# Six modulation chunks beside the linear attention: fp32 products replaced by products of fp32r parts, and a 4x2 matrix product in place of the turn

## The chip, the cores and the metric

One core of a Trainium2 chip runs the whole program. The metric is the device time in microseconds (us) of one execution. The engines are named as in the profile: PE (TensorE matmul), PEld (its weight load), DVE (VectorE), ACT (ScalarE), POOL (GpSimd) and SP (SyncE, which issues most of the loads).

## The reference, cut to what matters

Two transformer blocks on 512 tokens of width 1024 in float32. The first block takes its shifts, scales and gates from two conditioning vectors, `c` and `c_ctx`:

```
mod_x = (silu(c) @ w_ada[0] + b_ada[0])[:, None, :]      # w_ada: 1024 x 6144
mod_c = silu(c_ctx) @ w_ada[0] + b_ada[0]
sh1, sc1, g1, sh2, sc2, g2 = split(mod_x, 6)             # 1024 columns each
p_x = modulate(rmsnorm(h), sh1, sc1) @ w_in[0]           # also p_c, from ctx
... gla_bidir (4 heads, 2 directions, chunks of 64) ... pooling ...
h = h + g1 * (mix_x @ w_out[0])
h = h + g2 * moe(modulate(rmsnorm(h), sh2, sc2))         # top 4 of 32 experts
```

The second block (a retention and S5 mixer, differential attention, feed-forward layers) follows. `sh1` and `sc1` are needed at once. `g1`, `sh2`, `sc2` and `g2` are needed only from the output projection on, so the kernel computes most of them beside the linear attention.

## The kernel before, in words

**Modulations.** `w_ada` is cut into twelve chunks of 512 columns, c = 0 to 11. Each chunk comes in four loads of 512 KB (two blocks of 128 rows each). Chunks 0 to 3 come first. Chunks 4 to 9 are the ones that the change is about. Chunks 10 and 11 are computed in `out_pe`, at the start of the output projection. For a chunk `ada_pe` runs eight fp32 products: the stationary operand is `cc[:, k, :]` (128x2, the silu of both vectors), the moving one is the raw weight (128x512). The result is two rows of 512. `ada_act` copies them out of PSUM, `ada_pe` turns each 128 columns into a 128x2 block (four transposes of a 2x128 tile), and `add_ada` on DVE adds the bias.

**Parts.** Most other weights are used as fp32r parts. `conv_hi` (ACT, line 463) writes the high part of a unit of 128x1024 into one of four buffers of `wunits`. `conv_lo` (DVE, line 471) writes raw minus high over the raw weight in the ring. A high part may be written once PE has used the unit four places earlier, and a unit's ring slot is free for the next load once PE has used it.

**Ring.** SP loads the weights in the order in which they were planned into nine slots of 4 KB per partition. A load waits until PE has used what was in its slot, nine loads earlier. From the second half of `w_out` on, more slots come into use, and their first loads wait until POOL has finished its S5 tables (`"s5 parked"`).

**Steps.** The linear attention (`gla_pe`, `gla_act`, `gla_dve`) is four rounds (`ci` = 0 to 3: two pairs of heads, two directions). In each round every engine calls `step()` six times, at matching places. A step advances one generator of `jobs` and then one of `slow`, and each generator goes on to its next `yield`:

```
def step(self):
    if not self.advance(self.jobs) or self.pair:
        self.advance(self.slow)
```

The six places in a round are: before the turns of k (A), before the scores (B), before the masked product (C), after the first and after the second group of state products "u" (D, E), and before the output products "o" that read the states (F). DVE builds the states between the u products and the o products, with its steps at A, at B (before the mask), at C (before the decays of the next round), at D and E between the state updates, and at F after the decay products of the next round. The steps are numbered 1 to 24; after round 4 `finish_all` makes steps 25 and on, until both lists are empty. `jobs` holds the norm of the heads: DVE takes two reciprocals of 128x512 there, one in each of two steps.

The slow list is: pooling (steps 1 to 5), the S5 products (6 to 9), the modulation chunks 4, 5 and 6 (10 to 18, three steps each: two with four products each, one with the turn), the S5 turns (19 to 22), and the chunks 7, 8 and 9 (23 to 31). Instructions of an engine run in the order written, so a wait in a slow generator holds what stands behind it. PSUM banks are handed out in rotation, and a product waits until the former user of its bank has been read. In round 3 the last u products take the banks of the outputs of rounds 1 and 2, which the head norm frees on DVE.

After the linear attention `out_pe` runs chunks 10 and 11 and then the output projection; the router and the experts follow. ACT and DVE start on the parts of `w_out` after the barrier `"gla end"`.

Of the kernel before, what the change touches and what calls it, by code (L numbers as in the profile page):

```python
# [4 lines left out]
F32 = mybir.dt.float32  # L5
# [329 lines left out]
def build(nc, ins, out):  # L335
# [173 lines left out]
    for g in range(4):  # L509
        for h in range(2):  # L510
            W.plan(lambda g=g, h=h: I["ptab"][g, h * 256:(h + 1) * 256, :].rearrange("(j p) n -> p j n", p=128), 2, 512,
                   False)
    W.plan(lambda: I["w_pool"][0].rearrange("g c d -> c g d"), 4, 128, False)
    for c in range(4, 10):
        plan_cols(W, w_ada, 8, c * 512, 512, False)
    U_IN = len(W.units)
    plan_cols(W, w_ada, 8, 5120, 512, False)
    plan_cols(W, I["w_out"][0], 8, 0, 512)
# [359 lines left out]
    def ada_dve(v, c):  # L878
        yield
        yield  # L880
        add_ada(v, c)
        yield

    def add_ada(v, c):
        v.wait_ge(*pe("adat", c))
        v.own()
        v.inc(v.e.tensor_tensor(
            mcol[:, 4 * c:4 * c + 4, :], bank_of(("adat", c))[:, 0:8].rearrange("p (j s) -> p j s", s=2),
            C("bada", 4 * c, 4).unsqueeze(2).to_broadcast([128, 4, 2]), ALU.add), ("ada", c))
        v.free(("adat", c))  # L890

    RAW_ADA = [4 * FIRST.index(c) if c < 4 else 25 + 4 * (c - 4) for c in range(12)]

    def ada_row(c):
        return ar[0:2, c * 512:c * 512 + 512] if c < 4 else ar[0:2, 22272:22784]

    def mod_act(q):
        q.limit = U_IN
        q.wait_ge(*dve("all", "cols"))
        q.act(cc[:, :, 0], C("c", 0, 8), ACT.Silu)  # L900
        q.act(cc[:, :, 1], C("cctx", 0, 8), ACT.Silu, "silu c")
        sumsq_act(q, "x", hk, 8, 512, sq1)
        root2_act(q, "x", rx)
        sumsq_act(q, "ctx", lambda k: HC[:, k, :], 8, 256, sq1)
        root2_act(q, "ctx", rc)
        for h in range(2):
            for c in (h, h + 2):
                for _ in ada_act(q, c):
                    pass
            q.wait_ge(*dve("gm", h))  # L910
            for k in range(4 * h, 4 * h + 4):
                for s in range(2):
                    q.act((HXh, HCh)[s][:, k, :], normed_in(s, k), ACT.Identity, ("hn high", s, k), bias=M(0, k, s), scale=gm[:, k, s:s + 1])
            for u in (2 * h, 2 * h + 1):
                conv_hi(q, W, u)
# [18 lines left out]
            pass  # L934

    def mod_dve(v):
        v.limit = U_IN
        root1_dve(v, "x", 8, 512, rx, 1.0 / 1024)
        root3_dve(v, "x", rx)
        root1_dve(v, "ctx", 8, 256, rc, 1.0 / 1024)  # L940
        root3_dve(v, "ctx", rc)
        for k in range(8):
            v.stt(XN[:, k, :], hk(k), C("nmix", k), rx, ALU.mult, ALU.mult)
            v.stt(HC[:, k, :], HC[:, k, :], C("nmix", k), rc, ALU.mult, ALU.mult)
        for h in range(2):
            for c in (h, h + 2):
                for _ in ada_dve(v, c):
                    pass
            v.ts(gm[:, 4 * h:4 * h + 4, :], mcol[:, 8 + 4 * h:12 + 4 * h, :], 1.0, None, ALU.add, None, ("gm", h))
            ahead = None  # L950
            for k in range(4 * h, 4 * h + 4):
                for s in range(2):
                    v.ts(ntmp[s][k % 2], normed_in(s, k), gm[:, k, s:s + 1], M(0, k, s), ALU.mult, ALU.add)
                    if ahead:
                        hn_low(v, *ahead)
                    ahead = (s, k)
            hn_low(v, *ahead)
            for u in (2 * h, 2 * h + 1):
                conv_lo(v, W, u)
# [930 lines left out]
            yield  # L1890

    def out_act(q):
        q.limit = None
        for u in range(NUNIT):
            conv_hi(q, W, U_IN + u)
            split_act(q, "mix", mixp, lambda k: MX[:, k, :], range(2 * u, 2 * u + 2))
        q.wait_ge(*pe("ada", 10))
        q.copy(ada_row(10), bank_of(("ada", 10))[0:2, :], ("ada", 10))
        q.free(("ada", 10))
        q.slow += [last_ada_act(q), shift_act(q)]  # L1900
        tile = lambda c, m: q.jobs.append(tile_act(q, c * 4 + m))
        dense(q, conv_hi, W, [512], 8, tile)
        by_tiles(q, 1, tile)
        q.u += 4

    def out_dve(v):
        v.limit = None
        v.ts(gm2, mcol[:, 32:40, 0], 1.0, None, ALU.add, None)
        v.tt(gm2, gm2, C("nmlp", 0, 8), ALU.mult, "gm2")
        v.copy(S3[:, :, 0].bitcast(F32R), mcol[:, 24:32, 0])  # L1910
# [9 lines left out]
        v.u += 4  # L1920

    def out_pe(p):
        tails = [ada_pe(p, c) for c in (10, 11)]
        for x in tails:
            next(x)
# [1827 lines left out]
    def program_pe(p):  # L3753
# [3 lines left out]
        p.slow, p.pair = [s5_small_pe(p)], True  # L3757
        proj_pe(p)
        all_wait(p, "proj")
        p.slow += [pool_pe(p), s5_large_pe(p), ada_pe(p, 4), ada_pe(p, 5), ada_pe(p, 6), s5_turn_pe(p)]  # L3760
        p.slow += [ada_pe(p, c) for c in range(7, 10)]
        gla_pe(p)
        out_pe(p)
        p.pair = False
# [31 lines left out]
    def program_act(q):  # L3796
# [3 lines left out]
        q.slow, q.pair = [s5_small_act(q)], True  # L3800
        proj_act(q)
        all_wait(q, "proj")
        q.slow += [pool_act(q), s5_large_act(q), ada_act(q, 4), ada_act(q, 5), ada_act(q, 6), s5_turn_act(q)]
        q.slow += [ada_act(q, c) for c in range(7, 10)]
        gla_act(q)
        out_act(q)
        q.pair = False
# [35 lines left out]
    def program_dve(v):  # L3843
# [3 lines left out]
        v.slow, v.pair = [s5_small_dve(v)], True  # L3847
        proj_dve(v)
        all_wait(v, "proj")
        v.slow += [pool_dve(v), s5_large_dve(v), ada_dve(v, 4), ada_dve(v, 5), ada_dve(v, 6), s5_turn_dve(v)]  # L3850
        v.slow += [ada_dve(v, c) for c in range(7, 10)]
        gla_dve(v)
        out_dve(v)
        v.pair = False
# [132 lines left out]
```

## Time and profile before

| | us |
|---|---|
| median of 3 runs | 3272.61 (3269.02 to 3274.2) |
| the profiled execution, device time | 3273.05 |
| its span, first to last instruction | 3271.0 |
| PE busy | 3063.2 (94% of the span) |
| DVE busy | 2143.3 (66%) |
| ACT busy | 1645.5 (50%) |

The span is 2.05 us shorter than the device time of the same execution. The linear attention with what runs beside it takes the stretch from 206 to 358 us of the span; the output projection's products begin at 376.7 us.

### The profile page before, as it was taken

How to read it: one execution, taken by the hardware profiler on the slowest of the kernel's cores; microseconds unless marked ns; L12 is line 12 of the kernel's file. 1: busy time of each engine (PE TensorE's matmuls, PEld its weight loads, DVE VectorE, ACT ScalarE, POOL GpSimd, SP SyncE). 2: the span in 40 equal slices, each digit the busy share in tenths (PEclk: the TensorE clock that was granted, in tenths of full speed). 3: DMA queues.
4: the chain of work that ended last, by engine and by line, in shares of the span. 5: the costliest groups of instructions: out<-in, count | busy, mean ns of one | idle time of the engine just before them, and what ended most of it. 6: DMA issues, size and time to landing. Idle time of an engine off the chain costs nothing.

```text
span 3271.0 us, 37073 instructions
## 1 busy us (share of the span) xinstructions
PE 3063.2 (94%) x13794; PEld 2400.9 (73%) x13794; DVE 2143.3 (66%) x2483; ACT 1645.5 (50%) x1948; POOL 261.3 (8%) x234
## 2 busy tenths in 40 slices
PE   7989989999999999999979978999998987999998
PEld 3856467777777777777757756888886764888887
DVE  4555449999999999999966444443446457443446
ACT  2332328878887788878853212332335237432334
POOL 1053720000000000000010000000000000000000
PEclk8998969999999999999988978999999988999999
DMA  6244749999999999999963212223232210223210
GB/s 214 70 132 154 228 156 377 362 377 375 378 364 374 376 376 370 365 378 375 367 203 127 84 35 88 90 91 103 90 110 74 83 58 1 84 90 103 90 65 26
DMA packets 225086, 643.11 MB, mean 197 GB/s; under 512 B 20054, under 2 KB 38516, under 8 KB 224036
## 3 DMA queue, kind: packets, MB, share of 16 engines
q1 hardware_dynamic: 207984, 577.70, 48.7%
q0 software_dynamic: 12816, 51.39, 5.6%
q10 hardware_dynamic: 4100, 11.59, 0.9%
q8 instruction: 110, 1.80, 0.2%
q14 instruction: 76, 0.62, 0.1%
HBM read 608.10 MB, written 32.51 MB: 196 GB/s over the span
## 4 chain that ended last, share of the span: by engine, by line
PE 83%; DVE 11%; ACT 3%; issue 2%; DMA 1%; DVEq 0%; ACTq 0%; SPq 0%; POOLq 0%
PE ps L272 79%; PE ps L288 3%; DVE arena L203 2%; DVE arena L192 2%; ACT wunits L463 2%; DVE ring_r L471 1%; DVE arena L199 1%; ACT arena L237 1%; DVE arena L215 1%; DVE arena_r L203 1%; DVE arena L211 1%; DMA arena<-in_ctx 1%; DVE arena_r L471 1%; DVE arena L197 0%; DVE H L192 0%
## 5 line engine op out<-in xcount | busy, mean ns | idle before, releaser
L471 DVE TENSOR_TENSOR ring_r<-ring,wunits 128x1024 fp32r<-128x1024 f32 x795 | 948.7, 1218 | 660.2 <-ACT wunits L463 636.4
L463 ACT ACTIVATE wunits<-ring 128x1024 fp32r<-128x1024 f32 x795 | 834.6, 1054 | 809.0 <-PE ps L272 797.1
L272 PE MATMUL ps<-arena_r,wunits 128*128 128x512 f32 (+1 forms) x3552 | 1110.3, 394 | 12.4 <-DVE arena_r L192 6.9
L272 PE MATMUL ps<-wunits,arena_r 128*128 128x512 f32 x3520 | 991.3, 399 | 7.0 <-DVE arena_r L192 7.0
L272 PEld LDWEIGHTS ps<-arena_r,wunits 128*128 128x128 f32 x3552 | 671.4, 190 | 160.9 <-issue 16.6
L272 PEld LDWEIGHTS ps<-wunits,arena_r 128*128 128x128 f32 x3520 | 658.7, 189 | 152.2 <-DVE arena_r L192 8.8
L272 PE MATMUL ps<-arena_r,ring_r 128*128 128x512 f32 (+1 forms) x1776 | 694.8, 391 | 0.0
L272 PE MATMUL ps<-ring_r,arena_r 128*128 128x512 f32 x1280 | 410.3, 391 | 0.0
L272 PEld LDWEIGHTS ps<-arena_r,ring_r 128*128 128x128 f32 x1776 | 337.1, 190 | 70.4
L471 DVE TENSOR_TENSOR arena_r<-arena,wunits 128x1024 fp32r<-128x1024 f32 x240 | 284.9, 1221 | 16.6 <-ACT wunits L463 9.4
L463 ACT ACTIVATE wunits<-arena 128x1024 fp32r<-128x1024 f32 x240 | 254.3, 1061 | 65.6 <-PE ps L272 63.6
L272 PEld LDWEIGHTS ps<-ring_r,arena_r 128*128 128x128 f32 x1280 | 241.2, 188 | 53.1 <-issue 2.2
L272 PE MATMUL ps<-arena 128*128 128x128 f32 (+11 forms) x1074 | 192.4, 365 | 42.2 <-DVE arena L207 16.1
L237 ACT ACTIVATE arena<-ps 128x512 f32<-128x512 f32 (+6 forms) x190 | 121.3, 639 | 198.2 <-PE ps L272 144.9
L272 PEld LDWEIGHTS ps<-arena 64*128 64x128 f32 (+5 forms) x1074 | 135.0, 202 | 99.8 <-issue 41.4
L288 PE MATMUL ps<-KC,arena 128*128 128x128 f32 (+3 forms) x854 | 129.5, 294 | 82.5 <-DVE arena L203 43.5
L288 PEld LDWEIGHTS ps<-KC,arena 128*128 128x128 f32 (+3 forms) x854 | 104.1, 153 | 116.5 <-DVE arena L203 61.7
L272 PE MATMUL ps<-arena_r 128*128 128x512 f32 (+3 forms) x520 | 160.0, 392 | 0.9 <-DVE arena_r L197 0.9
L237 ACT ACTIVATE arena<-arena 128x512 f32<-128x512 f32 (+6 forms) x155 | 80.0, 516 | 134.1 <-DVE arena L192 84.1
L2360 POOL DMA_INDIRECT sum_scratch<-arena x33 | 52.3, 1586 | 1037.4 <-ACT arena L237 1037.4
L192 POOL TENSOR_TENSOR ring<-ring 128x512 f32<-128x512 f32 (+5 forms) x90 | 105.5, 1172 | 195.4 <-DVE ring L192 142.4
L192 DVE TENSOR_TENSOR arena<-ps,arena 128x512 f32<-128x512 f32 (+1 forms) x115 | 78.7, 684 | 61.3 <-PE ps L272 51.2
(171 smaller groups left out, 1936.1 us busy)
## 6 DMA issues: line engine op xcount, KB each, us to landing
ring<-in_w_gu SPq DMA_DIRECT2D x382, 512.0 KB, 8.5
ring<-in_w_down SPq DMA_DIRECT2D x170, 512.0 KB, 6.4
arena<-in_w_gu SPq DMA_DIRECT2D x146, 512.0 KB, 8.6
arena<-in_w_down SPq DMA_DIRECT2D x94, 512.0 KB, 6.4
ring<-in_w_ada SPq DMA_DIRECT2D x48, 512.0 KB, 4.5
ring<-in_ffn_w_gate SPq DMA_DIRECT2D x44, 512.0 KB, 3.5
ring<-in_ffn_w_up SPq DMA_DIRECT2D x44, 512.0 KB, 3.6
ring<-in_ffn_w_down SPq DMA_DIRECT2D x40, 512.0 KB, 3.6
```

The lines of the kernel that those rows point to most:

```text
L192: self.inc(self.e.tensor_tensor(o, x, y, op), key)
L199: self.inc(self.e.tensor_scalar(o, x, s1, s2, op0, op1), key)
L203: self.inc(self.e.scalar_tensor_tensor(out=o, in0=x, scalar=s, in1=y, op0=op0, op1=op1), key)
L211: self.inc(self.e.reciprocal(o, x), key)
L215: self.inc(self.e.tensor_reduce(o, x, AX.X, op), key)
L237: self.inc(self.e.activation(o, x, f, **kw), key)
L272: ins = self.e.matmul(o, l_, r_, start=start, stop=stop, skip_group_check=True)
L288: ins = self.e.transpose(o, x, self.ident[0:k, 0:k])
L463: q.inc(q.e.activation(h, raw, ACT.Copy), (st.tag, "hi", i))
L471: q.inc(q.e.tensor_tensor(lo, raw, h.bitcast(F32), ALU.subtract), (st.tag, "lo", i))
L2360: g.e.indirect_dma_start(out=sum_d, out_offset=bass.IndirectOffsetOnAxis(ap=idx, axis=0), in_=YB[i], in_offset=None, compute_op=ALU.add).t ...
```

## The change

Chunks 4 to 9 are planned as units (`split`), so ACT makes a high part and DVE a low part of each of their 24 pieces. The two vectors of `cc` are split as well: `CPARTS` holds for each block of 128 rows four columns, the high parts of both and the low parts of both. A chunk takes 16 fp32r products (128x4 stationary, 128x512 moving): the four columns with the weight's high part and with its low part. The result is four rows. The turn is four fp32 products of a 4x128 tile with `pick`, a 4x2 matrix that adds the row of high parts and the row of low parts. The high parts of the next chunk are written after the copy of the present one. For chunk 4 there are two more steps ahead, in which ACT and DVE make its first parts.

```diff
+    U_ADA = len(W.units)
     for c in range(4, 10):
-        plan_cols(W, w_ada, 8, c * 512, 512, False)
+        plan_cols(W, w_ada, 8, c * 512, 512)
     U_IN = len(W.units)
...
+    CPARTS = r(22816, 32, 4)
+    pick = ar[0:4, 22848:22850]
+    def ada4_pe(p, c):
+        if c == 4:
+            yield
+            yield
+        key = ("ada", c)
+        b = p.bank(key)
+        p.inuse.append(b)
+        if c == 4:
+            p.wait_ge(*dve("c parts"))
+        for j in range(4):
+            u = W.units[ada_unit(c, j)]
+            h, _, lo = unit_tiles(u)
+            p.wait_ge(*W.lo(u.i))
+            if j == 0:
+                p.claim(key)
+            for k in range(2):
+                kk = 2 * j + k
+                p.mm(PB[b][0:4, :], CPARTS[:, kk, :], h[:, k * 512:(k + 1) * 512], kk == 0, False)
+                p.mm(PB[b][0:4, :], CPARTS[:, kk, :], lo[:, k * 512:(k + 1) * 512], False, kk == 7, None, k == 1)
+            p.note((W.tag, "used", u.i))
+            if j == 1:
+                yield
+        p.note(key)
+        p.inuse.remove(b)
+        yield
+        b = p.bank(("adat", c))
+        p.wait_ge(*act("ada", c))
+        p.claim(("adat", c))
+        for j in range(4):
+            p.mm(PB[b][:, 2 * j:2 * j + 2], ar[0:4, 22272 + j * 128:22400 + j * 128], pick, j == 0, j == 3,
+                 ("adat", c) if j == 3 else None)
+        yield
+    def ada4_act(q, c):
+        def high(c, j0):
+            for j in range(j0, j0 + 2):
+                conv_hi(q, W, ada_unit(c, j))
+        if c == 4:
+            q.limit = U_IN
+            q.act(CPARTS[:, :, 0:2], cc, ACT.Copy, "c high")
+            high(c, 0)
+            yield
+            high(c, 2)
+            yield
+        yield
+        q.wait_ge(*pe("ada", c))
+        if c > 4:
+            q.wait_ge(*pe("adat", c - 1))
+        q.copy(ar[0:4, 22272:22784], bank_of(("ada", c))[0:4, :], ("ada", c))
+        q.free(("ada", c))
+        if c < 9:
+            high(c + 1, 0)
+        yield
+        if c < 9:
+            high(c + 1, 2)
+        yield
+    def ada4_dve(v, c):
+        def low(c, j0):
+            for j in range(j0, j0 + 2):
+                conv_lo(v, W, ada_unit(c, j))
+        if c == 4:
+            v.limit = U_IN
+            v.tt(pick, ident[0:4, 0:2], ident[0:4, 2:4], ALU.add)
+            v.wait_ge(*act("c high"))
+            v.tt(CPARTS[:, :, 2:4], cc, CPARTS[:, :, 0:2].bitcast(F32), ALU.subtract, "c parts")
+            yield
+            low(c, 0)
+            yield
+        low(c, 2)
+        yield
+        yield
+        if c < 9:
+            low(c + 1, 0)
+        add_ada(v, c)
+        yield
...
-        p.slow += [pool_pe(p), s5_large_pe(p), ada_pe(p, 4), ada_pe(p, 5), ada_pe(p, 6), s5_turn_pe(p)]
-        p.slow += [ada_pe(p, c) for c in range(7, 10)]
+        p.slow += [pool_pe(p), s5_large_pe(p), ada4_pe(p, 4), ada4_pe(p, 5), ada4_pe(p, 6), s5_turn_pe(p)]
+        p.slow += [ada4_pe(p, c) for c in range(7, 10)]
```

The slow lists of ACT and DVE change in the same way, and the counters of units at `mod_act`, `mod_dve`, `out_act`, `out_dve` and `out_pe` are set to the new numbering. The order of the loads and their sizes stay as they were.

## Rows read from the trace of the kernel before

**Rows 1.** The page's first part: busy time and share of each engine.
```profile
PE 3063.2 (94%) x13794; PEld 2400.9 (73%) x13794; DVE 2143.3 (66%) x2483; ACT 1645.5 (50%) x1948; POOL 261.3 (8%) x234
```
**Rows 2.** Windows of round 3 and the tail: length, PE, PEld, DVE, ACT, POOL, clock, DMA.
```profile
290.00:316.00 26.00, 20.23 (x93) 12.25 (x94) 20.48 (x26) 3.54 (x6) 1.20 (x2) 0.76 0.56 199
...
340.00:358.00 18.00, 16.64 (x45) 3.86 (x46) 12.55 (x10) 4.00 (x6) 17.22 (x11) 1.00 0.57 190
```
**Rows 3.** Timeline of PE, a chunk's products, fp32r triples and small products (start, length).
```profile
341.83 7.03 PE L272 MATMUL ps<-ring,SM 128*2 128x512 f32 x16
379.51 0.62 PE L272 MATMUL ps<-arena_r,wunits 128*128 128x512 f32 x2
379.96 0.39 PE L272 MATMUL ps<-arena_r,ring_r 128*128 128x512 f32 x1
380.19 0.62 PE L272 MATMUL ps<-arena_r,wunits 128*128 128x512 f32 x2
405.12 0.95 PE L272 MATMUL ps<-KC,arena 128*128 128x2 f32 x8
```
**Rows 4.** Groups by form, 236 to 377 us: the parts on DVE and ACT, the copy.
```profile
L471 DVE TENSOR_TENSOR ring_r<-ring,wunits 128x1024 fp32r<-128x1024 f32 x4 | 4.9, 1218 | 0.0
L463 ACT ACTIVATE wunits<-ring 128x1024 fp32r<-128x1024 f32 x4 | 4.2, 1044 | 0.7 <-DVE MOD L887 0.7
L237 ACT ACTIVATE arena<-ps 2x512 f32<-2x512 f32 x7 | 4.1, 586 | 33.2 <-PE ps L272 33.1
```
**Rows 5.** Timeline of PE, rounds 2 and 3; in brackets idle time and its releaser.
```profile
260.88 3.60 PE L272 MATMUL ps<-ring,SM 128*2 128x512 f32 x8
...
271.73 5.14 PE L272 MATMUL ps<-arena 64*128 64x64 f32 x32 [1.27 <-DVE arena L203]
276.81 5.09 PE L272 MATMUL ps<-ring,SM 128*2 128x512 f32 x8
...
306.36 1.22 PE L272 MATMUL ps<-arena 64*128 64x256 f32 x4 [4.64 <-DVE BPT L192]
...
309.22 6.29 PE L272 MATMUL ps<-arena 64*128 64x64 f32 x32 [1.13 <-DVE arena L203]
```
**Rows 6.** Timeline of DVE, rounds 2 and 3: decays, states, mask, head norm.
```profile
258.92 2.67 DVE L192 TENSOR_TENSOR arena<-arena 128x768 f32<-128x768 f32 x2
...
262.15 1.51 DVE L203 SCALAR_TENSOR_TENSOR arena<-arena,ps 128x256 f32<-128x256 f32 x3
...
289.07 1.58 DVE L1678 COPY_PREDICATED arena<-arena,ps 128x512 f32<-128x512 uint32 x2 [3.92 <-PE ps L272]
...
290.95 1.68 DVE L192 TENSOR_TENSOR arena<-arena 128x768 f32<-128x768 f32 x2
...
295.12 3.35 DVE L211 RECIPROCAL arena<-arena 128x512 f32<-128x512 f32 x1
...
302.22 3.35 DVE L211 RECIPROCAL BPT<-BPT 128x512 f32<-128x512 f32 x1
```
**Rows 7.** Timeline of PE, the end of round 4 and the tail.
```profile
336.26 3.39 PE L272 MATMUL ps<-arena 64*128 64x64 f32 x32
...
357.57 0.41 PE L288 MATMUL ps<-KC,arena 2*128 2x2 f32 x4 [0.68 <-ACT arena L237]
357.91 10.46 PE L272 MATMUL ps<-ring,SM 128*2 128x512 f32 x24
371.44 5.29 PE L272 MATMUL ps<-ring,SM 128*2 128x512 f32 x8 [3.07 <-DMA ring<-in_w_ada]
```
**Rows 8.** Timeline of POOL: its products, tables and the end of its S5 work.
```profile
258.26 31.40 POOL L192 TENSOR_TENSOR ring<-ring 128x512 f32<-128x512 f32 x24 [46.02 <-PE ps L272]
...
327.85 32.75 POOL L192 TENSOR_TENSOR ring<-ring 128x32 f32<-128x32 f32 x36
...
370.00 0.10 POOL L223 MEMSET ring<- 128x16 f32 x1 [8.52 <-DMA s_ww<-ring]
```

**Rows 9.** Timeline of ACT: the first part of the second half of `w_out`.
```profile
382.49 1.06 ACT L463 ACTIVATE wunits<-ring 128x1024 fp32r<-128x1024 f32 x1 [14.37 <-PE ps L272]
```

More of the change, by code:

```diff
@@ L882, in ada_dve, with ada_unit @@
         yield
+    CPARTS = r(22816, 32, 4)
+    pick = ar[0:4, 22848:22850]
+    def ada_unit(c, j):
+        return U_ADA + 4 * (c - 4) + j
+    def ada4_pe(p, c):
[30 more added lines that the diff above has]
+        yield
@@ L890, in add_ada @@
         v.free(("adat", c))
-    RAW_ADA = [4 * FIRST.index(c) if c < 4 else 25 + 4 * (c - 4) for c in range(12)]
+    RAW_ADA = [4 * FIRST.index(c) if c < 4 else 25 + 4 * (c - 10) for c in range(12)]
     def ada_row(c):
@@ L897, in mod_act @@
     def mod_act(q):
-        q.limit = U_IN
+        q.limit = U_ADA
         q.wait_ge(*dve("all", "cols"))
@@ L936, in mod_dve @@
     def mod_dve(v):
-        v.limit = U_IN
+        v.limit = U_ADA
         root1_dve(v, "x", 8, 512, rx, 1.0 / 1024)
@@ L1892, in out_act @@
     def out_act(q):
-        q.limit = None
+        q.limit, q.u = None, U_IN
         for u in range(NUNIT):
@@ L1906, in out_dve @@
     def out_dve(v):
-        v.limit = None
+        v.limit, v.u = None, U_IN
         v.ts(gm2, mcol[:, 32:40, 0], 1.0, None, ALU.add, None)
@@ L1922, in out_pe @@
     def out_pe(p):
+        p.u = U_IN
         tails = [ada_pe(p, c) for c in (10, 11)]
@@ L3802, in program_act @@
         all_wait(q, "proj")
-        q.slow += [pool_act(q), s5_large_act(q), ada_act(q, 4), ada_act(q, 5), ada_act(q, 6), s5_turn_act(q)]
-        q.slow += [ada_act(q, c) for c in range(7, 10)]
+        q.slow += [pool_act(q), s5_large_act(q), ada4_act(q, 4), ada4_act(q, 5), ada4_act(q, 6), s5_turn_act(q)]
+        q.slow += [ada4_act(q, c) for c in range(7, 10)]
         gla_act(q)
@@ L3849, in program_dve @@
         all_wait(v, "proj")
-        v.slow += [pool_dve(v), s5_large_dve(v), ada_dve(v, 4), ada_dve(v, 5), ada_dve(v, 6), s5_turn_dve(v)]
-        v.slow += [ada_dve(v, c) for c in range(7, 10)]
+        v.slow += [pool_dve(v), s5_large_dve(v), ada4_dve(v, 4), ada4_dve(v, 5), ada4_dve(v, 6), s5_turn_dve(v)]
+        v.slow += [ada4_dve(v, c) for c in range(7, 10)]
         gla_dve(v)
```

## Prediction

> **What bounds the kernel now.** I read the page first: PE is busy for 94% of the span [rows 1], so work taken from PE should be worth having, if PE is what the stage waits for. So next the windows of the linear attention: in round 3 (290 to 316 us) DVE is busy for 20.5 of 26 us and PE for 20.2, at a clock of 0.76 [rows 2]. The reader is to see that in this stretch DVE, not PE, has the fuller hand. The timeline of PE says the same by its waits: the last u products of round 3 wait 4.64 us and the o products of round 3 wait 1.13 us, both for DVE, and behind that wait the o products take 6.29 us where those of round 4 take 3.39 [rows 5, 7]. The clock explains this: 1.2 GHz after the idle time, 2.4 GHz in round 4. The timeline of DVE shows what it does meanwhile: mask, decays, two reciprocals of 3.35 us and the states, without a gap [rows 6]. After round 4 comes a tail, from 339.65 us (336.26 + 3.39) to 357.91, in which chunks 8 and 9 run bare on PE and only a copy of 0.6 us stands between them [rows 4, 7].
>
> **What the change takes off PE.** A chunk takes 7.03 us now, and three fp32r products of 512 columns take 0.68 us (379.51 to 380.19), so 0.227 each and 3.63 for sixteen [rows 3]. That is 3.4 us less a chunk, 20.4 for six. The new turn is not in the trace: at least the 0.41 of the present one [rows 7], at most the 0.95 of four fp32 products of 128 by 2 [rows 3]. I take 0.95, as it has the same instructions and no transposing; that gives back 3.2. Sum on PE: -17.2 us.
>
> **What it adds.** 24 high parts on ACT of 1.044 us (25.1) and 24 low parts on DVE of 1.218 us (29.2) [rows 4], in a stretch of about 100 us. The splitting of `cc` and `pick` are three small instructions, under 0.5 us on each engine, in step 10. The loads are the same and in the same order. ACT has room (4.0 of 18 us in the tail, 3.5 of 26 in round 3) [rows 2]. DVE has none in round 3. The order matters more than the sums: chunk 4 gets two empty steps, so every chunk comes two steps later on PE. Chunk 4 lies in steps 12 to 14, chunk 5 in 15 to 17, chunk 6 in 18 to 20, the S5 turns in 21 to 24, and chunk 7, which today lies within round 4, falls wholly behind it.
>
> **Round 2.** Nothing differs until 260.88 [rows 5]. Then PE has no chunk to fill steps 10 and 11 and ends its u products near 263. Its next step needs the first low part. DVE has three state updates until 263.7, four more (0.5 each [rows 6]), and then makes two low parts: PE gets them at 267.4 and 268.6. After 4.5 us idle I expect PE at 1.2 GHz, so chunk 4's first eight products take up to 3.4 us instead of 1.8, and the o products start near 270.8 and not at 271.73. At that clock they end near 276.5, the low parts of the second half come behind the decay products at 277.5 to 279, and chunk 4 ends at 280. Today the first half of chunk 5 ends at 281.9 (276.81 + 5.09) [rows 5]. So round 2 gains 2 us, with half a chunk less done.
>
> **Round 3.** On DVE the low parts of chunk 5 stand ahead of the mask and behind it, and the first ones of chunk 6 ahead of the last state updates. The mask today begins at 289.07 after 3.92 us idle, so that pair is half hidden (the mask starts at about 287.6, as PE is 2 us early), the two others are not. DVE then runs: mask to 289.2, two low parts to 291.7, decays to 293.4, states, first reciprocal and four states to about 302.5, second reciprocal to 307.4, two low parts to 310, last states by 312. On PE the turn of chunk 5 now takes the bank that the second head norm frees, near 307, the last u products stand behind it, and then the first half of chunk 6 (up to 3.4 us at 1.2 GHz) stands ahead of the o products. These start near 313.9, against 309.22 [rows 5]: 4.7 us later.
>
> **Round 4.** Today 339.65 - 309.22 = 30.4 us from these o products to the last ones' end, of which 7.0 are chunk 7. Without it 23.4; the second half of chunk 6 adds 1.8 to 3.4, its dearer turn 0.5, the low parts of chunk 7 ahead of the mask about 1.2. So 27.2, and the last o products end at 341.1 instead of 339.65: **+1.5 us**. PE's 3.4 us for each of chunks 4 to 6 are spent on waits for DVE and the lower clock.
>
> **The tail.** From that end T: chunk 7 (1.8), the head norm's sums (1.9), chunk 7's second half: T+5.9 with some delay of the squares on ACT behind the last S5 copies. Only then are the high parts of chunk 8 made, since they stand behind the copy of chunk 7. So each chunk is a chain over three engines: copy 0.6, high 1.04, low 1.22 four times, product 0.9, that is 7.6 us, which is no less than the 7.03 + 0.6 + 0.4 of today. DVE also does the head norm in the same steps. From its first reciprocal to its second lie 7.1 us, with four states (2.0) among them, so a half of the head norm is 4.9 [rows 6]; one half stands ahead of the low parts 8.2 and 8.3, the other ahead of 9.0. Chain: T+7.6 high part, T+10 two low parts, T+14.9 norm, T+17.4 two low parts, T+18.3 chunk 8; second norm until T+22.3, four low parts until T+27.2, products and copy T+28.8, turn and some twenty handovers of 0.05: T+30.8. Today it is 18.3. **+12 us** (12.5 rounded down, as the squares may not be late).
>
> **POOL beside it.** POOL computes on 128x512 tiles from 258.26 to 289.7 and again from 327.85 to 360.6 [rows 8]. Two 768-column differences on DVE take 2.67 us in the first stretch and 1.68 outside it [rows 6], 0.5 us more for each. Eight low parts stand one behind another in the tail, and POOL's second stretch starts about 9 us later than today (the S5 turns end two steps later) and so covers them all. Bounds: nothing, or 0.5 for each (+4). I take **+2.5**. The Trainium skill (page "SBUF — State Buffer", section "Who interferes with whom") says that a DVE instruction with two SBUF inputs and a POOL instruction that reads SBUF hold the shared ports in turns for a whole instruction. By that rule the low parts, whose inputs both lie in SBUF, would wait too; the pair of differences agrees (2.67 against 1.68), and the sum would be +4 instead of +2.5.
>
> **After the tail.** Today the last load of chunk 11 makes PE wait 3.07 us [rows 7]; after the change PE begins chunk 10 at 1.2 GHz (about +3) and that wait is covered: even. POOL's end, today at 370.00, lets the second half of `w_out` be loaded [rows 8], and it is first used at 382.49 [rows 9]: 12 us of room, while POOL slips by 9 to 15 and PE by 16. Everything behind follows PE. **Sum: 1.5 + 12 + 2.5 = +16 us.** Against the profiled 3273.05 that is 3289; this execution is 0.44 above the median of 3272.61, so **3288.6 us**.
>
> **Rivals.** *Chain of the tail shorter (no change that can be measured).* DVE waits less than I think in rounds 3 and 4 (T at 335) and POOL costs nothing: -4.7 + 12 = +7, and with the norms placed in the gaps of the copies (2.4 off each) +2: 3275 to 3280. For it speaks that DVE has much idle time ahead of round 3's mask [rows 6]; against it the instruction order. *PE's work decides (faster).* If the parts come early enough that PE never waits for one, -17.2 stands: 3255.4. It decides as soon as each low part is done before PE reaches its product; for it speak the 94% of PE [rows 1], against it the order in which the next chunk's high parts stand behind the present chunk's copy. *POOL and clock (slower still).* If each low part in the tail waits for a POOL instruction of about 1 us and PE stays at 1.2 GHz through chunks 8 to 10, +8 + 6 on top of 13.5: 3300.
>
> **From this to the numbers.** A measurement of this kernel tells about 0.2%, 6.5 us, from no change. Forecast (3280 to 3297): 0.58. No measurable change (3266 to 3279): 0.2. Faster, at PE's sum or part of it: 0.1. Slower still (3297 to 3305): 0.12. So slower 0.7, same 0.2, faster 0.1. Range 3268 to 3299: it leaves out the faster case and the end of the last one.
>
> **What would show it.** A chunk of 16 products with 3.6 us of PE where it isn't waiting; a wait of PE for DVE's line 471 before each half of chunks 8 and 9; reciprocals between low parts 8.1 and 8.2; the o products of round 3 near 314 and the end of round 4 near 341; chunk 10 near 374. Wrong it would be if DVE reached the low parts of chunk 8 ahead of the reciprocal's step, or if the products with four columns took another time than those with 128.

## The result, and the profile after

The changed kernel takes 3307.37 us (median; 3302.37 to 3316.61), the kernel before in the same session 3272.45. The ratio is 1.0108, with a 95% interval from 1.0091 to 1.0124. A second session of the same kernel gave 1.0113 [1.0094, 1.0132]. So the change costs 1.1%, some 35 us: the sign is the one forecast, the size is twice the 16 us. The profiled execution is the fastest of its runs (3302.37, span 3300.2) and lies 29.2 us above the span before.

The page's first part, after. PE is busy for only 4.7 us less than in [rows 1]; DVE and POOL are busy for 41.7 and 13.6 us more.
```profile
PE 3058.5 (93%) x13818; PEld 2401.7 (73%) x13818; DVE 2185.0 (66%) x2509; ACT 1669.1 (51%) x1973; POOL 274.9 (8%) x234
```
Groups of instructions by form of the changed kernel, from 255 to 388 us (DVE) and to 420 us (ACT): the low and the high parts. The high part costs what it did in [rows 4], 1042 against 1044 ns. The low part does not: its mean is 1802 ns where [rows 4] has 1218, so 24 of them take 42.3 us and not the 29.2 of the forecast.
```profile
L471 DVE TENSOR_TENSOR ring_r<-ring,wunits 128x1024 fp32r<-128x1024 f32 x24 | 42.3, 1802 | 7.7 <-ACT wunits L463 7.7
...
L463 ACT ACTIVATE wunits<-ring 128x1024 fp32r<-128x1024 f32 x29 | 28.7, 1042 | 20.1 <-PE ps L272 17.9 <-DVE MOD L976 2.2
```
Timeline of DVE after, in order: the low parts (pairs, L471), with the decay products (L203, 128x512) and the reciprocals between. The pairs beside POOL's first stretch take 3.49, 4.28, 4.01 and 2.64 us, and those of the tail 3.21, 5.12, 5.89 and 4.22. Undisturbed, a pair is 2.35 (the row at 320.53). The reciprocals stand at 3.35 everywhere, as in [rows 6].
```profile
265.67 3.49 DVE L471 TENSOR_TENSOR ring_r<-ring,wunits 128x1024 fp32r<-128x1024 f32 x2
...
273.74 3.11 DVE L203 SCALAR_TENSOR_TENSOR arena<-arena 128x512 f32<-128x512 f32 x2
276.77 4.28 DVE L471 TENSOR_TENSOR ring_r<-ring,wunits 128x1024 fp32r<-128x1024 f32 x2
...
287.19 4.01 DVE L471 TENSOR_TENSOR ring_r<-ring,wunits 128x1024 fp32r<-128x1024 f32 x2
...
293.06 2.64 DVE L471 TENSOR_TENSOR ring_r<-ring,wunits 128x1024 fp32r<-128x1024 f32 x2
...
307.83 3.35 DVE L211 RECIPROCAL BPT<-BPT 128x512 f32<-128x512 f32 x1
...
319.19 1.42 DVE L203 SCALAR_TENSOR_TENSOR arena<-arena 128x512 f32<-128x512 f32 x2
320.53 2.35 DVE L471 TENSOR_TENSOR ring_r<-ring,wunits 128x1024 fp32r<-128x1024 f32 x2
...
354.44 3.21 DVE L471 TENSOR_TENSOR ring_r<-ring,wunits 128x1024 fp32r<-128x1024 f32 x2 [2.80 <-ACT wunits L463]
...
357.95 3.35 DVE L211 RECIPROCAL arena<-arena 128x512 f32<-128x512 f32 x1
...
362.74 5.12 DVE L471 TENSOR_TENSOR ring_r<-ring,wunits 128x1024 fp32r<-128x1024 f32 x2
367.89 3.35 DVE L211 RECIPROCAL BPT<-BPT 128x512 f32<-128x512 f32 x1
...
372.67 5.89 DVE L471 TENSOR_TENSOR ring_r<-ring,wunits 128x1024 fp32r<-128x1024 f32 x2
...
378.77 4.22 DVE L471 TENSOR_TENSOR ring_r<-ring,wunits 128x1024 fp32r<-128x1024 f32 x2
```
Timeline of POOL after. Its two stretches are 5.2 and 7.3 us longer than in [rows 8]: the contention is mutual. The second begins at 340.75 and ends at 380.77, so seven of the tail's eight low parts start beside it; the last one runs from 381.78 and takes 1.21.
```profile
256.84 36.63 POOL L192 TENSOR_TENSOR ring<-ring 128x512 f32<-128x512 f32 x24 [46.02 <-PE ps L272]
...
340.75 40.02 POOL L192 TENSOR_TENSOR ring<-ring 128x32 f32<-128x32 f32 x36
```
Instruction by instruction (the timeline of both engines in windows of 0.1 us), three of POOL's products of the tail and the low part that starts beside each of them:
```profile
372.12 2.45 POOL L192 TENSOR_TENSOR ring<-ring 128x1024 f32<-128x1024 f32 x1
372.67 2.98 DVE L471 TENSOR_TENSOR ring_r<-ring,wunits 128x1024 fp32r<-128x1024 f32 x1
...
374.65 2.82 POOL L192 TENSOR_TENSOR ring<-ring 128x1024 f32<-128x1024 f32 x1
375.58 2.98 DVE L471 TENSOR_TENSOR ring_r<-ring,wunits 128x1024 fp32r<-128x1024 f32 x1
...
377.55 3.22 POOL L192 TENSOR_TENSOR ring<-ring 128x1024 f32<-128x1024 f32 x1
378.77 3.09 DVE L471 TENSOR_TENSOR ring_r<-ring,wunits 128x1024 fp32r<-128x1024 f32 x1
```
The three low parts end 1.08, 1.09 and 1.09 us after the end of the POOL product beside them (375.65 against 374.57, 378.56 against 377.47, 381.86 against 380.77). Alone a low part takes 1.22 us. So each stands until the POOL product under way is done and then takes 1.1 us more. It becomes 1.8 to 1.9 us longer here. Beside the products of 512 columns in the first stretch (1214 ns each in the kernel before) the low parts become 0.3 to 1.1 longer.
Timeline of PE after: first product with chunk 4's parts, o products of rounds 2, 3 and 4, chunk 7's turn, chunk 8's second half and its turn, then chunks 10 and 11 with the wait for the last load. (An fp32 product stands in the trace as two entries, an fp32r product as one; so 24 entries are chunk 10 and half of chunk 11.) A product of fp32r parts with 512 columns takes 0.23 us from start to start at 2.4 GHz and 0.43 at 1.2 GHz, whether its stationary tile has 4 columns or 128; a turn takes 1.05 and 1.86.
```profile
267.31 0.58 PE L272 MATMUL ps<-wunits,arena_r 128*4 128x512 f32 x1 [6.05 <-DVE ring_r L471]
...
271.01 3.67 PE L272 MATMUL ps<-arena 64*128 64x64 f32 x32
...
319.32 3.41 PE L272 MATMUL ps<-arena 64*128 64x64 f32 x32
...
340.68 3.98 PE L272 MATMUL ps<-arena 64*128 64x64 f32 x32 [0.62 <-DVE arena L203]
...
353.45 1.05 PE L272 MATMUL ps<-arena 4*128 4x2 f32 x8 [0.68 <-ACT arena L237]
...
365.07 0.59 PE L272 MATMUL ps<-wunits,arena_r 128*4 128x512 f32 x1 [5.50 <-DVE ring_r L471]
...
370.45 1.86 PE L272 MATMUL ps<-arena 4*128 4x2 f32 x8 [0.68 <-ACT arena L237]
...
387.95 12.00 PE L272 MATMUL ps<-ring,SM 128*2 128x512 f32 x24
405.30 4.99 PE L272 MATMUL ps<-ring,SM 128*2 128x512 f32 x8 [5.35 <-DMA ring<-in_w_ada]
```
The last o products end at 344.66 (339.65 before), chunk 10 starts at 387.95 (357.91, [rows 7]) and is turned at 415.91 (382.32 before). The waits of PE between 240 and 420 us, summed by what ended them, say what that time was:
```profile
PE ps L272 <- DVE ring_r L471: 26.0, 11, 6.0
PE ps L272 <- DVE BPT L192: 6.3, 1, 6.3
PE ps L272 <- DVE arena L192: 5.6, 1, 5.6
PE ps L272 <- DMA ring<-in_w_ada: 5.4, 1, 5.4
```
With three small groups these waits are 47.3 us; the same view of the kernel before sums to 12.0. So PE waits 35.3 us longer in a stage that became 35.0 longer (173.9 from the o products of round 1 to the turn of chunk 10, against 138.9). PE's own work did not shrink, since 68 of the 96 new products ran at the lower clock, at 0.2 us more each: 13.6 us. The windows of round 3 and of the tail show the granted clock (the last three figures are clock, DMA share and GB/s); [rows 2] has a clock of 0.76 and 1.00 in such stretches.
```profile
290.00:319.00 29.00, 16.14 (x68) 8.66 (x66) 25.79 (x30) 9.89 (x13) 4.80 (x5) 0.71 0.49 164
...
345.00:388.00 43.00, 26.52 (x77) 10.10 (x76) 29.51 (x18) 12.18 (x15) 34.16 (x30) 0.58 0.50 168
```

### The profile page after: what moved, and what is told of

The parts are those of the page before. It is cut to its first block, busy times and chain, and to the rows that moved or that the text cites. A ratio compares the mean times of both kernels' runs of the same rounds, so it can differ in the third digit from the quotient of the medians.

```text
span 3300.2 us, 37185 instructions
## 1 busy us (share of the span) xinstructions
PE 3058.5 (93%) x13818; PEld 2401.7 (73%) x13818; DVE 2185.0 (66%) x2509; ACT 1669.1 (51%) x1973; POOL 274.9 (8%) x234
## 4 chain that ended last, share of the span: by engine, by line
PE 81%; DVE 12%; ACT 3%; issue 2%; DMA 1%; DVEq 0%; ACTq 0%; SPq 0%; POOLq 0%
PE ps L272 78%; PE ps L288 3%; DVE ring_r L471 2%; DVE arena L203 2%; DVE arena L192 2%; ACT wunits L463 2%; DVE arena L199 1%; ACT arena L237 1%; DVE arena L211 1%; DVE arena L215 1%; DMA arena<-in_ctx 1%; DVE arena_r L203 0%; DVE H L192 0%; DVE arena L197 0%; DVE arena_r L471 0%
## 5 line engine op out<-in xcount | busy, mean ns | idle before, releaser
L471 DVE TENSOR_TENSOR ring_r<-ring,wunits 128x1024 fp32r<-128x1024 f32 x819 | 992.6, 1237 | 669.8 <-ACT wunits L463 646.6
L463 ACT ACTIVATE wunits<-ring 128x1024 fp32r<-128x1024 f32 x819 | 858.0, 1054 | 812.7 <-PE ps L272 799.1
L272 PE MATMUL ps<-wunits,arena_r 128*128 128x512 f32 (+1 forms) x3568 | 1017.7, 401 | 33.1 <-DVE ring_r L471 26.0
L272 PEld LDWEIGHTS ps<-wunits,arena_r 128*128 128x128 f32 (+1 forms) x3568 | 663.1, 187 | 194.8 <-DVE ring_r L471 33.9
L272 PE MATMUL ps<-ring_r,arena_r 128*128 128x512 f32 (+1 forms) x1328 | 436.7, 396 | 0.0
L471 DVE TENSOR_TENSOR arena_r<-arena,wunits 128x1024 fp32r<-128x1024 f32 x240 | 285.2, 1221 | 16.7 <-ACT wunits L463 8.6
L272 PEld LDWEIGHTS ps<-ring_r,arena_r 128*128 128x128 f32 (+1 forms) x1328 | 245.9, 185 | 61.2 <-issue 9.1
L272 PE MATMUL ps<-arena 128*128 128x128 f32 (+12 forms) x1122 | 201.1, 361 | 49.1 <-DVE arena L192 18.4
L237 ACT ACTIVATE arena<-ps 128x512 f32<-128x512 f32 (+7 forms) x190 | 121.4, 639 | 215.8 <-PE ps L272 167.8
L272 PEld LDWEIGHTS ps<-arena 64*128 64x128 f32 (+6 forms) x1122 | 141.5, 199 | 110.2 <-issue 44.6
L192 POOL TENSOR_TENSOR ring<-ring 128x512 f32<-128x512 f32 (+5 forms) x90 | 118.1, 1312 | 193.8 <-DVE ring L192 140.9
```

The source lines that it names most:

```text
L192: self.inc(self.e.tensor_tensor(o, x, y, op), key)
L237: self.inc(self.e.activation(o, x, f, **kw), key)
L272: ins = self.e.matmul(o, l_, r_, start=start, stop=stop, skip_group_check=True)
L463: q.inc(q.e.activation(h, raw, ACT.Copy), (st.tag, "hi", i))
L471: q.inc(q.e.tensor_tensor(lo, raw, h.bitcast(F32), ALU.subtract), (st.tag, "lo", i))
```

## The experiments

Theory A: DVE's low parts are longer beside POOL's products than forecast, in the tail and in the rounds. Rival B: the order (high part behind the copy, head norm between the low parts) costs more steps than counted. Rival C: the clock. Each run is read by three lengths of the profile: the rounds (start of the o products of round 1 to the end of the last o products), the tail (from there to chunk 10), and chunk 10 to its turn. Times in us; the ratio is to the kernel before.

| kernel | rounds | tail | chunk 10 to turn | median | ratio [95%] |
|---|---|---|---|---|---|
| before | 96.2 | 18.3 | 24.4 | 3272.45 | |
| changed | 102.6 | 43.3 | 28.0 | 3307.37 | 1.0108 [1.0091, 1.0124] |
| changed, second session | 102.2 | 42.2 | 27.6 | 3309.19 | 1.0113 [1.0094, 1.0132] |
| no second POOL stretch | 102.2 | 32.3 | 28.1 | 3299.99 | 1.0062 [1.0041, 1.0082] |
| short first POOL stretch | 96.2 | 43.1 | 27.5 | 3307.55 | 1.0098 [1.0082, 1.0113] |
| before, no second POOL stretch | 96.2 | 18.3 | 27.6 | 3278.14 | 1.0018 [1.0008, 1.0028] |
| no low parts | 90.3 | 18.3 | 19.5 | 3483.65 | 1.0625 [1.0605, 1.0645] |
| before, two empty steps | 90.1 | 28.2 | 23.2 | 3278.37 | 1.0001 [0.9991, 1.0010] |
| 4 to 6 in parts | 100.7 | 26.1 | 22.7 | 3282.47 | 1.0017 [1.0006, 1.0029] |
| 7 to 9 in parts | 90.9 | 42.9 | 29.9 | 3295.37 | 1.0059 [1.0043, 1.0074] |
| parts made before the copy | 105.6 | 38.3 | 30.5 | 3308.85 | 1.0103 [1.0088, 1.0118] |
| only 4 in parts, in gaps | 93.6 | 19.9 | 24.1 | 3274.25 | 1.0005 [0.9996, 1.0015] |
| only 7, 8 in parts, in gaps | | | 19.5 | 3267.76 | 0.9984 [0.9975, 0.9994] |
| 4, 7, 8 in parts, in gaps | | | 19.5 | 3263.84 | 0.9964 [0.9952, 0.9975] |

Each ratio is to the kernel before beside it on the same chip (its median lay between 3272.5 and 3276.9), so kernels are compared by the ratio. (In the last two, chunk 7 lies within round 4, so the rounds and the tail are not cut at the same place.)

**No second POOL stretch.** The changed kernel without POOL's 36 table products.
```diff
-        while m_ < 64:
+        while m_ < 1:
```


> This is the changed kernel, but POOL leaves out the 36 products of its second stretch (the S5 tables, so those tables aren't computed). In the profile of the changed kernel the eight low parts of chunks 8 and 9 took 18.4 us beside them instead of 8 x 1.22. Theory A (each low part waits for a POOL instruction): the pairs fall to about 2.4 us, the tail from the last o products to chunk 10 from 43.3 to about 34 us, the time to about 3298 us. Rival B (the tail is long because of its order and the 1.2 GHz clock, POOL matters little): tail at most 3 us shorter, time 3304 us or more.

The tail falls by 11.0 us to 32.3. Timeline of DVE: the tail's pairs are back at 2.35.
```profile
354.15 2.36 DVE L471 TENSOR_TENSOR ring_r<-ring,wunits 128x1024 fp32r<-128x1024 f32 x2 [2.80 <-ACT wunits L463]
...
361.60 2.35 DVE L471 TENSOR_TENSOR ring_r<-ring,wunits 128x1024 fp32r<-128x1024 f32 x2
...
371.33 2.36 DVE L471 TENSOR_TENSOR ring_r<-ring,wunits 128x1024 fp32r<-128x1024 f32 x2
```
18.44 us of low parts became 9.42: 9.0 of the 11.0. The other 2.0 stand beside a higher clock (0.76 against 0.58 from 345 to 388 us) and are not taken apart further. In the profiled run chunk 10 is turned 11.3 us sooner, counted from the o products of round 1. The ratio falls from 1.0108 to 1.0062, which is 15 us; as the intervals of the two are 11 and 13 us wide, the total agrees with the 11 us and doesn't say more. PE waits 0.97 and 4.92 us for the last loads. The rounds, with POOL's first stretch left in, don't move.

**Short first POOL stretch.** The changed kernel with 3 of the 24 products that POOL computes first.
```diff
-        for s_ in range(8):
+        for s_ in range(7, 8):
```


> The changed kernel, but POOL leaves out 21 of the 24 products of its first stretch (they are 128x512 and run from 257 to 293 us; the last of the eight groups stays, so the S5 powers are not all computed). Three pairs of low parts took 3.49, 4.28 and 4.01 us beside them. Theory A: they fall to about 2.4 each, the o products of round 3 begin about 4 us earlier (315.3 instead of 319.3), time 3 to 4 us below the changed kernel. Rival: the rounds are held by the head norm and the banks, and the o products of round 3 begin less than 1 us earlier.

Now the rounds fall by 6.4 us and the tail doesn't. Timeline of DVE: pairs of the rounds at 2.35, the tail's third pair at 5.89, to the hundredth what it was.
```profile
274.01 2.35 DVE L471 TENSOR_TENSOR ring_r<-ring,wunits 128x1024 fp32r<-128x1024 f32 x2
...
368.11 5.89 DVE L471 TENSOR_TENSOR ring_r<-ring,wunits 128x1024 fp32r<-128x1024 f32 x2
```
The o products of round 3 start 71.0 us after those of round 1 (77.3 in the changed kernel). Chunk 10 is turned 7.0 us sooner, counted from round 1, and the first store of the experts' results is made 4.4 sooner. The total neither shows the gain nor excludes it: the ratio is 1.0098 against 1.0108, that is 3 us less, with intervals that overlap, and the four runs spread from 3304 to 3314. The profiled run is the slowest of them. From that first store to its end, where the edit changes nothing, it takes 2748.2 us, and the profiled run of the changed kernel (its fastest) 2734.4: 13.8 us of scatter, more than the edit's effect.

The 6.4 us are not all the low parts' own. The four pairs beside POOL's first stretch become 5.0 us shorter (14.42 to 9.41), but the decays and decay products of round 2 become shorter too (2.89 and 3.11 to 1.69 and 1.42), and the kernel before pays for those as well (2.93 and 2.89 in its timeline). The control, the kernel before with the short stretch, was not run, so how the 6.4 us divide is not shown.

**Before, no second POOL stretch.** The control: the same edit as in the first experiment, in the kernel before.

> The kernel before with POOL's second stretch left out as in the first experiment (the S5 tables aren't computed). It shows how much of the 11 us that the changed kernel got back in its tail is the low parts' own. Theory A: in the kernel before DVE has few instructions with two SBUF operands in the tail, so the tail stays within 1 us of 18.3 and the time within 0.2% of before. Rival (POOL slows this stretch in both kernels): tail 3 us shorter or more.

Timeline of PE: the last o products and the turn of chunk 9 stand where [rows 7] has them.
```profile
336.25 3.39 PE L272 MATMUL ps<-arena 64*128 64x64 f32 x32
...
357.56 0.41 PE L288 MATMUL ps<-KC,arena 2*128 2x2 f32 x4 [0.68 <-ACT arena L237]
```
So POOL's second stretch costs the tail nothing as long as DVE has no low parts there. The time rises by 0.2%: PE waits for the last loads of chunk 11 (1.77 and 4.27 us), as it does in the first experiment. SP issues these four loads at the same times as in the kernel before (from 356.92 and 356.93 on). But POOL's own loads for the router now start at 358.75 instead of 370.56, and SP's next loads of `w_out` at 363.65 instead of 370.13. The slowest of the last loads of `w_ada` lands 13.0 us after its issue instead of 9.9. That the loads beside them are the cause fits, but was not tried by itself.

**No low parts.** Leaves out the 24 low parts (the calls of `conv_lo` for these chunks are gone too) and reads the high parts in their place. Left as they are: all products, copies, turns and high parts.
```diff
-            p.wait_ge(*W.lo(u.i))
+            p.wait_ge(*W.hi(u.i))
...
-                p.mm(PB[b][0:4, :], CPARTS[:, kk, :], lo[:, k * 512:(k + 1) * 512], False, kk == 7, None, k == 1)
+                p.mm(PB[b][0:4, :], CPARTS[:, kk, :], h[:, k * 512:(k + 1) * 512], False, kk == 7, None, k == 1)
```


> The changed kernel without the 24 low parts on DVE: the second product of each pair reads the high part again (so the low parts' contribution is left out), and PE waits for ACT alone. PE and ACT do the same work as in the changed kernel. Theory A (DVE's instructions on the chain are the loss): last o products end near 335 us, tail 43 - 18 - 4 = about 25 us plus waits for the high parts, time about 3278 us. Rival B (clock and order): 3295 us or more.

Its modulations are others, and the experts' part then reads other blocks (647 MB from HBM in all instead of 608), so the total tells nothing here; the stage does. Timeline of PE: the last o products and chunk 10.
```profile
330.10 3.39 PE L272 MATMUL ps<-arena 64*128 64x64 f32 x32 [0.68 <-DVE arena L203]
...
351.79 13.89 PE L272 MATMUL ps<-ring,SM 128*2 128x512 f32 x32
```
The tail is 18.3 us, the same as before (25 were expected): DVE's low parts, with all that hangs on them, are 25 us of the tail and 12 of the rounds. POOL's share is in these, and so is the clock's: without the low parts PE has a granted clock of 1.00 from 333 to 352 us, with them 0.58 in the tail.

**Before, two empty steps.** The kernel before, with the change's two steps ahead of chunk 4 and nothing else.
```diff
-        p.slow += [pool_pe(p), s5_large_pe(p), ada_pe(p, 4), ada_pe(p, 5), ada_pe(p, 6), s5_turn_pe(p)]
+        p.slow += [pool_pe(p), s5_large_pe(p), empty(2), ada_pe(p, 4), ada_pe(p, 5), ada_pe(p, 6), s5_turn_pe(p)]
```


> The kernel before, with nothing but two empty steps ahead of chunk 4 on the three engines, so that each chunk and the S5 turns come two steps later and chunk 7 falls behind round 4. Theory A: round 4 is bound by PE, so the 7 us of chunk 7 only move from it into the tail; POOL ends some 8 us later, which is covered; 3272 to 3276 us. Rival D (the two steps themselves are a good part of the loss, as PE has nothing in steps 10 and 11): 3280 us or more.

Rounds 6.1 us shorter, tail 9.9 longer (chunk 7 now lies in it): 3.8 us at chunk 10, of which 1.2 come back by its turn. In the total they don't show (1.0001).

**4 to 6 in parts, and 7 to 9 in parts.** The first has chunks 7 to 9 as before, the second chunks 4 to 6, both with the two steps.
```diff
-        plan_cols(W, w_ada, 8, c * 512, 512)
+        plan_cols(W, w_ada, 8, c * 512, 512, c in SPLIT)
```


> Chunks 7 to 9 are fp32 products as before, 4 to 6 stay in parts at the places of the changed kernel. If the tail has most of the loss (theory A): last o products end near 343 us as in the changed kernel, tail about 26 us with chunk 7 in it (18.3 of before + 7.0), time about 3283 us. Rival C (the rounds have most of it): time 3295 us or more.

> Chunks 4 to 6 are fp32 products (behind the two empty steps, so at the places of the changed kernel), chunks 7 to 9 in parts as in the changed kernel; the first parts of chunk 7 are made at the turn of chunk 6. Theory A (low parts on DVE cost where they stand on the chain, in the rounds about 10 us, in the tail about 25): the last o products end near 335 us (332.6 with all chunks plain and the two steps), the tail is about 43 us as in the changed kernel, chunk 10 near 378, time about 3293 to 3298 us. Rival (the tail is only long because it inherits lateness from the rounds): tail under 35 us, time under 3288 us.

The parts of 4 to 6 lengthen the rounds (100.7 against 90.1 with the two steps alone), those of 7 to 9 the tail (42.9 against 28.2). In the total the first half of the change costs 0.17%, the second 0.59%.

**Parts made before the copy.** The changed kernel with each high part ahead of the copy of the chunk before, and each low part a step earlier (of the edit only ACT's half is shown; DVE's `low` moves in the same way).
```diff
+        if c < 9:
+            high(c + 1, 0)
         yield
+        if c < 9:
+            high(c + 1, 2)
         q.wait_ge(*pe("ada", c))
```


> The changed kernel, but the parts of the next chunk are made while PE still multiplies the present one (high parts ahead of the copy, low parts a step earlier). The number of instructions is the same. If the order (high parts behind the copy) is what makes the tail long: tail from 43 to about 30 us, time about 3294 us. If DVE's own work is (eight low parts at 1.2 to 2.9 us and two halves of the head norm at 4.9, together about 28 us): tail no shorter than 36 us, time 3300 us or more; the rounds unchanged within 2 us.

B has a small share: the tail is 5.0 us shorter, the rounds 3.0 longer, which was not expected, and the total stays. Timeline of DVE: four low parts in a row take 12.03 us beside POOL, 3.0 each.
```profile
352.98 6.44 DVE L471 TENSOR_TENSOR ring_r<-ring,wunits 128x1024 fp32r<-128x1024 f32 x4
...
369.41 12.03 DVE L471 TENSOR_TENSOR ring_r<-ring,wunits 128x1024 fp32r<-128x1024 f32 x4
```

**The changed kernel again.**

> The changed kernel once more, beside the three others on one chip: 3300 to 3312 us, rounds 102 to 103 us from the o products of round 1 to the end of round 4, tail 43 us, if the profile shown is typical.

The window of its tail has the clock at 0.69 where the first profile has 0.58, and the tail is 42.2 against 43.3. The low parts in it are shorter by as much (17.30 against 18.44 us for the four pairs), so these two profiles show no price of the clock beyond that. No run changes the clock alone: C stays untested as a cause of its own. The granted clock in the tail is 1.00 where PE doesn't wait for low parts (before, and without them) and 0.58 to 0.76 where it does, and 36 of the 68 slower products lie in the tail, some of them on the chain behind the last low part of a chunk.
```profile
345.00:388.00 43.00, 24.72 (x79) 8.31 (x78) 31.68 (x23) 13.12 (x16) 34.21 (x31) 0.69 0.52 172
```

**Parts in DVE's gaps.** The places of before (no empty steps), and only the chunks whose parts fit where DVE is idle: those of chunk 4 in round 1, of chunk 7 ahead of the mask of round 4, of chunk 8 behind the last states. Chunks 5, 6 and 9 stay as before.
```diff
+    HI_AT = {2: [(4, 0), (4, 1)], 3: [(4, 2), (4, 3)], 18: [(7, 0), (7, 1), (7, 2), (7, 3)], 23: [(8, 0), (8, 1)], 24: [(8, 2), (8, 3)]}
+    LO_AT = {3: [(4, 0), (4, 1)], 4: [(4, 2), (4, 3)], 19: [(7, 0), (7, 1), (7, 2), (7, 3)], 24: [(8, 0), (8, 1)], 25: [(8, 2), (8, 3)]}
```


> The kernel before, with only chunks 4, 7 and 8 in parts, at the places of before and without the two empty steps; their low parts are put into gaps of DVE: chunk 4's in round 1, where DVE waits 3.7 and 2.7 us for PE, chunk 7's ahead of the mask of round 4 (9.0 us of waiting), chunk 8's at the end of round 4. Theory A says that the same products then gain: 3.4 us each in round 2, in round 4 and in the tail, less 0.5 for each turn, so chunk 10 some 8 us earlier than before (350 instead of 358), time about 3265 us. Rival (fp32r products with parts don't pay in this stretch wherever the parts are made, because of the 1.2 GHz clock or the ring): 3272 us or more.

> Only chunk 4 in parts, its low parts in DVE's gaps of round 1. In the kernel with chunks 4, 7 and 8 in parts the o products of round 3 began 3.3 us earlier than before (1.4 us of it after taking out the start of round 2, see the result). If each chunk gives what PE saves on it where PE is what is waited for: the o products of round 2 about 3 us earlier, of which a part is lost at the lower clock and in round 3; time 3269 to 3273 us. Rival: the gain of that kernel is chunk 4's: 3266 us or less.

> Only chunks 7 and 8 in parts, chunk 7's low parts ahead of the mask of round 4, chunk 8's at the end of round 4. PE is busy without a gap there, so the theory expects 3.4 us for chunk 7 in round 4 and about 2 us for chunk 8 in the tail (3.4 less a turn of 0.5 to 1 and the lower clock), and the first store of the experts' results 5 to 8 us earlier than before: 3266 to 3270 us. Rival (the parts of chunk 8 come too late, PE waits for them): 3271 us or more.

With all three chunks the time is 0.36% below the kernel before, with chunks 7 and 8 alone 0.16%, with chunk 4 alone it can't be told from it (3269 to 3273 us were forecast): there the rounds are 2.6 us shorter and the tail is 1.7 longer. Timeline of DVE, with all three: the low parts outside POOL's stretches cost 1.16 to 1.18 each, and those that fall into POOL's second stretch (from 323.33 on) only 1.28 and 1.5.
```profile
231.97 2.36 DVE L474 TENSOR_TENSOR ring_r<-ring,wunits 128x1024 fp32r<-128x1024 f32 x2 [0.78 <-ACT wunits L466]
...
309.33 4.63 DVE L474 TENSOR_TENSOR ring_r<-ring,wunits 128x1024 fp32r<-128x1024 f32 x4
...
328.17 2.56 DVE L474 TENSOR_TENSOR ring_r<-ring,wunits 128x1024 fp32r<-128x1024 f32 x2
...
333.76 2.99 DVE L474 TENSOR_TENSOR ring_r<-ring,wunits 128x1024 fp32r<-128x1024 f32 x2
```
From round 1 to the start of chunk 10 this kernel is 4.5 us shorter than before, and from there to the turn 4.9 (19.5 against 24.4): PE no longer waits for the last load of chunk 11. Why that load lands in time here was not tried.

## Why the prediction was right in its direction and wrong in its size

**What the change takes off PE, what it adds on ACT: right.** Sixteen products take 3.6 us where PE isn't waiting and has its full clock (0.23 each); the turn is 1.05 where 0.95 was taken; high parts 1042 ns.

**Round 2: the order right, the times met by luck.** PE got the first low part at 267.31 (forecast 267.4) and the o products started at 271.01 (270.8). But this profile stands 1.4 us earlier from round 1 on. Counted from the o products of round 1, the first low part came 1.3 us later than forecast and the o products of round 2 1.6 (29.0 against 27.4). With POOL's first stretch cut it is 27.7. The second half of chunk 4 then came late as well, with the pair of 4.28 us.

**Round 3: the order right, the price of the low parts not.** The o products start 77.3 us after those of round 1, on the clock of the kernel before at 320.7, against 313.9. With POOL's first stretch cut they start at 71.0, that is 314.4: the forecast to half a microsecond. The 6.3 us between go with POOL's first stretch. That the agreement is so close is partly luck, since the cut also shortens the decays, which the forecast had at the length they have beside POOL.

**Round 4: a little too dear.** 25.3 us from these o products to the end of the last, 27.2 were forecast. This hides 1.9 us of the lateness of the rounds.

**The tail: right as far as it goes.** The reciprocals stand between the low parts as forecast, and the tail without POOL is 32.3 against 30.8, with the dearer turns and the lower clock in it.

**POOL beside it: the step that failed.** The prediction took +2.5 us, with +4 as the upper bound, from 0.5 for each low part of the tail and none for the rounds. Taking POOL's stretch away gave 11.0 us in the tail (9.0 of it the low parts' own, 18.44 against 9.42, 1.1 for each) and 6.3 to 6.4 in the rounds (5.0 of it the low parts' own lengthening, the rest not divided). Two mistakes made it. The bound came from the pair of differences with 768 columns, 0.5 us dearer beside POOL's products of 1.2 us. The second stretch was read as products of 128x512 too; it has 36 products of 32 to 1024 columns, and chunks 8 and 9 meet the longest. Groups by form of POOL in the changed kernel, 250 to 390 us:
```profile
L192 POOL TENSOR_TENSOR ring<-ring 128x1024 f32<-128x1024 f32 x6 | 16.4, 2728 | 0.5
```
And the rounds were left out, though [rows 8] puts POOL's first stretch over chunk 4's and chunk 5's parts. In the trace low parts and decay products with two SBUF inputs slow down beside POOL (3.11 for two decay products against 1.42), the reciprocal with one stays at 3.35, three state updates, which read one of their two tiles from PSUM, take 1.51 inside POOL's first stretch [rows 6] as outside it, and POOL's own stretches grow by 5.2 and 7.3 us. The Trainium skill (page "SBUF — State Buffer", section "Who interferes with whom") says that a DVE instruction with two SBUF inputs contends with a POOL instruction that reads SBUF, and that the port pair they share is an exclusive lock. The trace agrees, down to the low parts that end 1.08 to 1.09 us after POOL's product. The prediction had this rule and gave it 0.5 us for each part.

An estimate from [rows 8] with one mean POOL product as the wait of each low part is 8 x 1.31 us in the rounds (31.40/24) and 8 x 0.91 in the tail (32.75/36), 17.8 in all against 17.3 measured. That the sum fits is luck in part: 10.5 stand against 6.3, and 7.3 against 11.0, because which products a part meets decides. The rival "POOL and clock" had the tail right (about 1 us for each part, and PE at the lower clock from the middle of chunk 8 on), not the rounds.

**After the tail: forecast even, +3.6.** Chunk 10 begins at the lower clock, so the 24 entries of chunks 10 and 11 take 12.00 against 10.46, and the wait for the last load is 5.35 and not covered (3.07 before).

**The sum.** Counted to the turn of chunk 10: rounds +6.4 (forecast +1.5), tail +25.0 (+14.5), after it +3.6 (0), less 1.4 for an earlier start: +33.6 against +16. Until the end 4.4 come back in the profiled run, which gives 29.2. So of the 17.6 us that the forecast was short, 4.9 are in the rounds, 10.5 in the tail and 3.6 after it, less the 1.4. The share of each cause is shown for the low parts as a whole (no low parts: 25 and 12) and for POOL in the tail (11, with a control). In the rounds the 6.4 of POOL lack their control. That POOL's tail share holds 2.0 us which are not the low parts' own is not explained further, and the clock's own share is open.

## What to carry to other kernels

A part that DVE makes from two SBUF inputs must be priced by what POOL runs at the same time: read POOL's stretches, and the size of the products in them, against the place of each such instruction. Take the length of the POOL instruction that it meets as the upper bound of its wait (in the changed kernel up to 1.9 us beside products of 2.18, up to 1.1 beside products of 1.21), and do so for every stretch, not only the one in which the chain is bare. Work moved off a busy PE is worth only what PE doesn't wait for afterwards: here the sum of 17 us for PE turned into 35 us more of waits, and the lower clock took most of the 17 back. In this kernel the same conversion pays where DVE is idle: with three chunks of six converted, and their parts in DVE's gaps, it is 0.36% faster than the kernel before. So convert the chunks that find a gap, and not all.

## What was not expected of the hardware

- A low part of 128x1024 takes 1.22 us alone (a pair 2.35) and up to 3.1 beside POOL's products in the changed kernel (four in a row 12.03 with the parts made early): it ends 1.08 to 1.09 us after the POOL product that it meets. POOL's products of 1024 columns rise from 2178 to 2728 ns meanwhile.
- An fp32r product of 512 columns takes 0.23 us with a stationary tile of 4 columns as with one of 128, and the four fp32 products of a turn with the 4x2 matrix take 1.05 us at 2.4 GHz and 1.86 at 1.2 GHz.
- Taking POOL's table products away lets other loads start sooner, and the last loads of chunk 11, issued at the same times in the kernel before, then come later (PE waits 1.77 and 4.27 us for them instead of 3.07). In the changed kernel there is hardly a difference (0.97 and 4.92 against 5.35).
